# A residual kept turned in four PSUM banks through 32 expert steps of a decoder trunk

## The reference, cut to what matters

```python
h = h + y @ w_out
h = h + moe(rmsnorm(h, g_ffn), w_r, b_r, w1, b1, w2, b2)
gate = sigmoid(rmsnorm(h, g_ple) @ w_pg + b_pg)
h = h + gate * (p @ w_pp)                  # p: 256 per token
y_out = rmsnorm(h, g_final)

def moe(xt, ...):                          # top 4 of 32 experts
    combine = softmax_of_top4(xt @ w_r + b_r)
    for e in range(32):
        hdn = xt @ w1[e] + b1[e]           # 1024 -> 2048
        act = (clip(up) + 1) * min(gate, 7) * sigmoid(1.702 * gate)
        out += combine[:, e] * (act @ w2[e] + b2[e])   # 1024 -> 1024
```

## Time and profile before

| what | value |
|---|---|
| median of 3 runs | 1093.55 us (1091.79 to 1093.87) |
| the profiled execution | 1091.18 us, its span 1089.5 us |
| PE busy | 97% of the span |
| DVE, ACT, POOL busy | 35%, 15%, 1% |
| moved by DMA | 426.80 MB, mean 392 GB/s |
| mean granted clock of PE | 0.998 of full speed |

### The profile page before, as it was taken

The page is one execution under the profiler, slowest core; times in us unless marked ns, Lnnn a source line. Parts: engine busy times, 40 slices in busy tenths (PEclk is TensorE's granted clock), DMA queues, the critical chain, the costliest instruction groups (busy, mean ns, idle before and its releaser), DMA issues.

```text
span 1089.5 us, 13468 instructions
## 1 busy us (share of the span) xinstructions
PE 1061.2 (97%) x5250; PEld 429.7 (39%) x5250; DVE 385.1 (35%) x875; ACT 168.2 (15%) x298; POOL 13.8 (1%) x20
## 2 busy tenths in 40 slices
PE   9999999999999999999999999999999999999996
PEld 7884433444333333333333333333333333333342
DVE  6563743222333333333333333333333332333326
ACT  2550600010000000000000000000000000000034
POOL 0100200000000000000000000000000000000000
PEclk9999999999999999999999999999999999999999
DMA  9957699998999999999999999999999999999941
GB/s 281 354 216 300 262 401 428 424 397 374 395 431 430 433 431 433 430 428 434 427 432 433 426 434 425 432 430 431 431 437 426 434 430 431 433 422 430 423 182 40
DMA packets 34312, 426.80 MB, mean 392 GB/s; under 512 B 5383, under 2 KB 8655, under 8 KB 16493
## 3 DMA queue, kind: packets, MB, share of 16 engines
q1 hardware_dynamic: 34284, 426.41, 93.6%
HBM read 424.57 MB, written 1.43 MB: 391 GB/s over the span
## 4 chain that ended last, share of the span: by engine, by line
PE 76%; DMA 22%; DVE 1%; ACT 0%; SPq 0%; issue 0%; DVEq 0%
PE bank L1669 29%; DMA ring<-in_w 21%; PE bank L1710 17%; PE bank L1344 5%; PE bank L1599 5%; PE bank L1581 3%; PE bank L1432 3%; PE bank L1607 2%; PE bank L1592 2%; PE bank L1689 2%; PE bank L1767 1%; PE bank L1779 1%; DMA w_in<-in_w_in 1%; PE bank L1695 1%; PE bank L1654 1%; PE bank L1534 1%
## 5 line engine op out<-in xcount | busy, mean ns | idle before, releaser
L1669 PE MATMUL bank<-ring,xgT 128*64 128x512 f32 x2048 | 447.5, 593 | 14.5 <-DMA ring<-in_w 14.5
L1669 PEld LDWEIGHTS bank<-ring,xgT 128*64 128x64 f32 x2048 | 145.5, 137 | 298.3 <-issue 267.6
L1710 PE MATMUL bank<-ring,actT 128*64 128x512 f32 x1024 | 233.6, 598 | 0.0
L1177 DVE TENSOR_SCALAR gmin<-bank 128x512 f32<-128x512 f32 x32 | 22.1, 692 | 338.9 <-PE bank L1669 338.9
L1710 PEld LDWEIGHTS bank<-ring,actT 128*64 128x64 f32 x1024 | 67.9, 136 | 141.4 <-issue 120.5
L700 ACT ACTIVATE sig<-gmin 128x512 f32<-128x512 f32 x32 | 20.1, 630 | 446.4 <-DVE gmin L1177 446.4
L1131 DVE TENSOR_TENSOR h<-bank,h 128x512 f32<-128x512 f32 x132 | 84.8, 684 | 8.7 <-PE bank L1599 7.6
L1085 DVE TENSOR_TENSOR xgT<-bank,vecT 128x512 f32<-128x512 f32 x32 | 22.1, 692 | 155.9 <-PE bank L1592 155.2
L1171 DVE TENSOR_SCALAR wpick<-slot_no,pos,share 128x128 f32<-128x128 f32 (+1 forms) x96 | 27.1, 339 | 112.5 <-PE bank L1669 112.5
L1599 PE MATMUL bank<-y,wpickT 64*128 64x512 f32 x264 | 65.6, 615 | 0.8 <-ACT y L711 0.8
L711 ACT ACTIVATE y<-bank 128x512 f32<-128x512 f32 x32 | 19.1, 597 | 237.5 <-PE bank L1710 237.5
(11 more groups left out here) (306 smaller groups left out, 645.6 us busy)
## 6 DMA issues: line engine op xcount, KB each, us to landing
ring<-in_w SPq DMA_DIRECT2D x53, 4096.0 KB, 32.0
ring<-in_w SPq DMA_DIRECT2D x86, 2048.0 KB, 28.4
w_in<-in_w_in SPq DMA_DIRECT2D x3, 2048.0 KB, 14.2
w_out<-in_w_out SPq DMA_DIRECT2D x1, 4096.0 KB, 17.0
w_pg<-in_w_pg SPq DMA_DIRECT2D x4, 1024.0 KB, 26.7
h<-in_x_prompt SPq DMA_DIRECT2D x2, 512.0 KB, 3.9
w_in<-in_w_in SPq DMA_DIRECT2D x2, 512.0 KB, 7.8
w_in<-in_w_in SPq DMA_DIRECT2D x1, 1024.0 KB, 10.8
```

Of the source, the lines that this page charges most:

```text
L1669: ins = pe.matmul(bank[part][r, :], xgT[:, (k % FOUR) * W1_QUADS + k // FOUR, :], w[:, c:c + HALF], start=False, stop=(k == W1_SLOTS - 1), ...
L1710: ins = pe.matmul(bank[2][CAP * m:CAP * (m + 1), :], actT[:, half:half + CAP], pair[:, c:c + HALF], start=(f == 0), stop=(f == FF // P - 1 ...
```

## The change: the residual turned, in PSUM

What it does. At step 0 PE turns the prompt's residual by 16 plain matmuls with the identity (`residual_in`) into banks 4 to 7: channels on the partitions, eight blocks of 128, two blocks of 256 tokens in a bank. These banks stay open: each later `scatter` has `y` as the stationary operand (128 channels wide) and `wpickT` moving (256 tokens), eight matmuls that accumulate onto the residual. The eight samples are turned by `samples_in` and kept in SBUF (`hT_samples`); their products, eight matmuls of 8 columns, go to free columns of banks 0 and 2, and DVE adds them there (two additions of 128x32), for which PE waits ahead of the second matrix. The embedding is made turned, after step 3 alone, in eight blocks of 264 tokens. The gate is made turned: `w_pg` is the stationary operand, `tail_nT` moves, eight blocks. `b_pg` and `g_final` become columns of `vecT` (two more short loads at the start). The final norm's sums over channels are reduced by DVE over blocks and by PE over partitions; the rows are turned back at the end by 24 transposes (`turn_back`) into banks that have come free, and ACT and DVE scale them by the token's factor as they evict.

```diff
-    GATE_BANKS = (0, 2, 4)
+    GATE_BANKS = (0, 1, 2, 0, 1, 0, 1, 0)
+    GATE_BEFORE = (None, None, None, 0, 1, 3, 4, 5)
-    EMBED_STEPS = (2, 3)
+    EMBED_STEP = 3
+        def residual(b):
+            return bank[RESIDUAL + b // 2][:, (b % 2) * SEQ:(b % 2 + 1) * SEQ]
 # SP
-            load(bpg[:], a["b_pg"][0].partition_broadcast(P), rows_in)
-            load(gfin[:], a["g_final"].partition_broadcast(P), rows_in)
 # ACT, step
                 act.wait_ge(wpick_turned, i + 2)
-                act.wait_ge(spread, i * NT + NT)
+                act.wait_ge(spread, i * 2 + 2)
+                act.wait_ge(h_added, i + NT + 2)
                 act.activation(wpickT[:], bank[0][:, 0:T], ACT.Copy).then_inc(wpickT_ready, 1)
...
+                    act.activation(y[:, left], bank[2][:, left], ACT.Copy).then_inc(y_ready, 1)
+                    act.activation(y[:, right], bank[2][:, right], ACT.Copy).then_inc(y_right_ready, 1)
 # ACT, tail
+            for j in range(2):
+                act.wait_ge(spread, n * 2 + 1 + 3 * j)
+                for b in (2 * j, 2 * j + 1):
+                    act.activation(tail_nT[:, b, 0:SEQ], residual(b), ACT.Identity, scale=vcol("g_ple", b))
+            for j in (0, 1, 2, 3):
+                act.activation(squares[:, 2 * j:2 * j + 2, 0:SEQ], bank[RESIDUAL + j][:]..., ACT.Square)
+            for b in range(KD - 1):
+                sigmoid_of(b)
+                if b > 0:
+                    square_and_scale(b - 1)
+            square_and_scale(KD - 2)
+            sigmoid_of(KD - 1)
...
 # DVE, step
-                add_tile(0, P, 4, i * NT + 1, i * 2 * NT + NT)
-                add_tile(1, P, 6, i * NT + 2, i * 2 * NT + NT + 2)
+                add_samples(i * 2 + 2, i + NT + 1)
                 if not last:
                     make_xgT(i + 1, gathered_turned)
-                add_samples(4, i * NT + 3, i * 2 * NT + NT + 4)
 # DVE, add_samples
+                dve.tensor_tensor(samples_wide[:, 0:four], bank[0][:, T:T + four], samples_wide[:, 0:four], ALU.add)
+                dve.tensor_tensor(samples_wide[:, four:], bank[2][:, 0:four], samples_wide[:, four:], ALU.add
+                                  ).then_inc(h_added, 1)
 # DVE, tail
+            dve.tensor_reduce(token_sums[:, 0, :], squares[:].rearrange("p b t -> p t b"), AX.X, ALU.add)
+            link(dve.reciprocal(rstd_wide[:], rstd_wide[:]))
+            def normal(b):
+                dve.wait_ge(plegate_made, b + 1)
+                dve.tensor_tensor(gate[:, b, :], bank[GATE_BANKS[b]][:, 0:T], rstd_wide[:], ALU.mult)
+            def add_embedded(b):
+                dve.wait_ge(plegate_ready, b + 1)
+                link(dve.tensor_tensor(gate[:, b, :], gate[:, b, :], pwT[:, b, :], ALU.mult))
+                dve.tensor_tensor(gate[:, b, SEQ:T], gate[:, b, SEQ:T], hT_samples[:, b, :], ALU.add)
+                dve.tensor_tensor(gate[:, b, 0:SEQ], gate[:, b, 0:SEQ], residual(b), ALU.add).then_inc(h_final, 1)
+            for b in range(KD - 1):
+                normal(b)
+                if b > 0:
+                    add_embedded(b - 1)
+            add_embedded(KD - 2)
+            dve.tensor_reduce(token_sums[:, 1, :], squares[:, 0:KD - 1, :].rearrange("p b t -> p t b"), AX.X, ALU.add)
+            normal(KD - 1)
+            add_embedded(KD - 1)
...
 # PE
-                    ins = pe.matmul(bank[first_bank + m][0:rows, :], wpickT[r, t * P:t * P + rows], y[r, :],
-                                    start=True, stop=True)
+            def residual_in():
+                for b in range(KD):
+                    for t in range(2):
+                        pe.matmul(residual(b)[:, t * P:(t + 1) * P], h[:, t, b * P:(b + 1) * P], ident[:],
+                                  start=(b % 2 == 0 and t == 0), stop=False, skip_group_check=True)
+            def scatter(blocks=range(KD // 2), last=False):
+                for c in blocks:
+                    for m in range(2):
+                        r, b = slice(CAP * m, CAP * (m + 1)), KD // 2 * m + c
+                        ins = pe.matmul(residual(b), y[r, c * P:(c + 1) * P], wpickT[r, 0:SEQ], start=False, stop=last,
+                                        skip_group_check=True)
+            def scatter_samples(blocks=range(KD // 2)):
+                for c in blocks:
+                    for m in range(2):
+                        r = slice(CAP * m, CAP * (m + 1))
+                        at_c = (0 if m else T) + c * NS
+                        ins = pe.matmul(bank[2 * m][:, at_c:at_c + NS], y[r, c * P:(c + 1) * P], wpickT[r, SEQ:T],
+                                        start=True, stop=True, skip_group_check=True)
 # PE, step
+                if type(i) is int and i == EMBED_STEP + 1:
+                    pe.wait_ge(pw_ready, KD)
...
-                pe.wait_ge(h_added, i * 2 * NT + NT)
-                scatter(0, P, 4)
-                scatter(1, P, 6)
+                if started:
+                    samples_in()
+                    residual_in()
+                scatter()
...
-                pe.wait_ge(h_added, i * 2 * NT + NT + 2)
                 for t, rows in TILES:
                     ins = pe.transpose(bank[0][:, t * P:t * P + rows], wpick[0:rows, t, :], ident[0:rows, 0:rows])
                 ins.then_inc(wpick_turned, 1)
-                scatter_samples(4)
+                scatter_samples()
+                pe.wait_ge(h_added, i + NT + 2)
                 pe.wait_ge(actT_ready, i + 1)
 # PE, tail
+            scatter(range(2), True)
+            scatter_samples()
+            scatter(range(2, 4), True)
+            for b in range(KD):
+                for j, k in enumerate((0, 4, 1, 5, 2, 6, 3, 7)):
+                    ins = pe.matmul(bank[GATE_BANKS[b]][:, 0:T], w_pg[:, k, b * P:(b + 1) * P], tail_nT[:, k, :],
+                                    start=(j == 0), stop=(j == KD - 1), skip_group_check=True)
```

More of the change, by code:

```diff
@@ L782, in _ @@
+            act.wait_ge(rows_back, 2 * KD)
+            for m in range(2):
+                ins = act.activation(y_out[0:NS, 2, halves(m)], bank[BACK_BANKS[2][m]][0:NS, :], ACT.Copy,
+                                     scale=rstd[0:NS, 2:3])
+            ins.then_inc(y_final, 1)
         @block.vector
@@ L1123, in _, with add_samples @@
                 make_shares(r)
-            def add_tile(t, rows, first_bank, products, added):
+            samples_wide = hT_samples[:].rearrange("p k s -> p (k s)")
+            def add_samples(products, added):
                 dve.wait_ge(spread, products)
                 dve.wait_ge(h_added, added)
-                for m in range(2):
-                    src = bank[first_bank + m]
-                    dve.tensor_tensor(h[0:rows, t, halves(m)], src[0:rows, :], h[0:rows, t, halves(m)], ALU.add
-                                      ).then_inc(h_added, 1)
@@ new lines, in _ @@
+            dve.tensor_scalar(scaled[:, KD - 1, :], gate[:, KD - 1, :], vcol("g_final", KD - 1), None, ALU.mult
+                              ).then_inc(scaled_dve, 1)
+            dve.wait_ge(rms_ready, 6)
+            link(dve.reciprocal(rstd[:, 0:2], rms[:, 0:2]))
+            dve.wait_ge(rms_ready, 7)
+            dve.reciprocal(rstd[0:NS, 2:3], rms[0:NS, 2:3]).then_inc(rstd_ready, 1)
+            dve.wait_ge(rows_back, 2 * KD - 1)
+            for t in range(2):
+                dve.tensor_scalar(y_out[:, t, halves(1)], bank[BACK_BANKS[t][1]][:], rstd[:, t:t + 1], None, ALU.mult
+                                  ).then_inc(y_right_final, 1)
@@ new lines, in scatter @@
+            def scatter(blocks=range(KD // 2), last=False):
[4 more added lines that the diff above has]
+                                        skip_group_check=True)
+                        if last and c % 2:
+                            ins.then_inc(spread, 1)
+                if not last:
+                    ins.then_inc(spread, 1)
@@ L1771, in _ @@
[L1771 to L1781 removed]
+            pe.wait_ge(h_added, n + NT + 1)
@@ new lines, in _ @@
+            turn_back(5)
+            turn_back(6)
+            pe.wait_ge(h_final, 6)
+            for b in range(4):
+                turn_back_samples(b)
+            pe.wait_ge(plebias_ready, KD)
+            for b in range(4, KD - 1):
+                turn_back_samples(b)
+            pe.wait_ge(sums_ready, 2)
+            last_sums(token_sums[:, 1, :], True)
+            pe.wait_ge(sums_ready, 3)
+            last_sums(squares[:, KD - 1, :], False).then_inc(last_sums_made, 1)
+            turn_back(KD - 1)
```

408 lines of the change are left out of this document (170 added, 238 removed).

## The result

The changed kernel takes **1096.74 us** (median of 8 runs, 1095.57 to 1098.61), the kernel before beside it 1094.05 (8 runs): ratio 1.0028, 95% interval 1.0017 to 1.0039. A second set of runs gave 1096.23 against 1093.35, ratio 1.0029 (1.0019 to 1.0040). So it is slower by 2.7 to 2.9 us, a little over what can be told from no change. The forecast was 1095.0, range 1090.5 to 1104.0.

A forecast was written before the change was run, and what follows sets the result against it. PE was taken to bound early steps, the 430 GB/s weight stream from step 5 on, carrying early lateness. Loop +4.8 and tail -3.3 give +1.5 us on the median of 1093.55: 1095.0, range 1090.5 to 1104.

The forecast's parts named there:

- d: Time the change adds to each PE step: scatter -0.1, samples -0.05, new wait +0.8, together 0.65 us (0.4 to 0.9).
- Single work: Steps 0 to 3: residual and samples' turns add 5.1 us, the embedding saves 3.55, so 1.55 us later.
- The loop's end: Last step starts 4.8 us later by the weight stream: 1.55 + 5 x 0.65; 4.7 by PE.
- 5d: PE's added time per step, counted for five early steps only, carried by the weight stream to the loop's end: 5 x 0.65.
- rival C: In mid-step, short products' halves don't pair: about 1124 us (samples), 1146 (scatter), 1175 (both); chance 0.05.
- rival B: PE bounds every step once its added time exceeds the slack of 0.65 us; 1099.7 at 0.8, 1104.5 at 0.95; chance 0.22.
- The tail: From the copy of the last y to the end: 47.7 us before, 44.4 forecast, 3.3 sooner.
- The overhang of 2.2: DVE's work between gate blocks 6 and 7, 6.1 us with a reduction; block 7 covers 3.9, 2.2 stick out.
- rival E: Tail reductions reading 264 elements apart are slow; at twice the time per element, 2.1 us more, 1097.1; chance 0.09.
- The finish: Work after the last gate block, from normalisation through evictions to store and end: 8.7 us.
- D: Faster: the finish falls under the last gate block, the tail saves 7.3 us, 1091.0; chance 0.17.
- the frame: Kernel before's median of 1093.55 us, 2.4 above its profiled execution of 1091.18; the forecast was put on that median.

The follow-up runs named there:

- the runs with doubled products: Kernel before with the samples' products of every step made twice, both halves (1104.0 us, ratio 1.0092) or one half only (1103.0 us, ratio 1.0087).
- the run with 0.22 us added: Kernel before with two of the three turns of the next `wpick` made twice in every step: 1094.55 us, ratio 1.0010.
- the running sum: Changed kernel with the last reduction replaced by DVE adding each block's square to a sum between gate blocks: 1094.40 us, ratio 1.0007 to the kernel before.
- filled wait: Changed kernel with one more matmul between the samples' products and PE's wait for DVE's additions: 1097.19 us, ratio 1.0029 to the kernel before.
- late start: Kernel before with five more filler matmuls ahead of step 0: 1098.11 us against 1093.28, ratio 1.0045.

## Why the prediction was right

The direction, the size within 1.8 us and the main path were right: lateness of the first steps, carried by the stream, against a shorter tail. Point by point:

**The step, d = 0.65: measured 0.60.** The scatter saved nothing where 0.1 was expected; the samples run in pairs (1.02 against 0.96), as the runs with doubled products show from the other side (264 products on alternating halves took 62.3 us, 198 with two of three on one half 62.0). The wait was laid out at 0.8 with its first weight load; idle time is 0.48 to 0.56, since the second addition starts 0.11 us behind the first and not 0.2. The Trainium skill's rule on weight loads (TensorE: Matmul & The Clock Gate, LDWEIGHTS (loading the stationary operand)) gave an estimate of 1.7 us for the sixteen in series; the trace has 1.02, so they were not in series. The Trainium skill (TensorE: Matmul & The Clock Gate, Part 3: Packing small matmuls — row/col tiling, The mechanism) tells that products on different row groups overlap, and the trace agrees with its 1.02.

**Single work and the first five steps: 4.8, measured 4.45** (step 5 against step 0, 153.71 against 149.27), of it 1.45 of single work, where 1.55 was laid out, and 5 x 0.60.

**The loop's end was mis-sized: 4.8, measured 7.05 to 9.25.** The term that failed is 5d. It should have been some 8d to 9.5d: the run with 0.22 us added shows 1.70 from step 0 to the last step (884.78 against 883.08), 7.7 x 0.22; moving the samples gave 8.8 x 0.78; and the changed kernel itself has 7.05 - 1.45 = 9.3 x 0.60. Two of the steps more are shown: they lie behind the last wait for the ring, where PE's own pace counts again (0.43 more in the run with 0.22 added; in the running sum 1.26 more, 2.1 x 0.60). The rest, one step in the run with 0.22 added and 2.4 in the running sum (its last wait for the ring ends 686.71 us after step 5's start, before 685.26), is lateness that the stream takes on after step 5's start. The prediction's own row had this: DMA still idles in 280 to 290 us, which is inside step 5, and yet only the steps ahead of it were counted; after the change the share there is 0.72, before it 0.83. How many steps have a part in it was not taken apart. With 1.55 + 8.5 x 0.60 the forecast of the loop's end would have been 6.65. (The times given for rival C are one to three us above its own formula, 1122.8 for d = 1.55; nothing hangs on it.)

**Two bounds of equal length.** From step 5 to the last step the stream needs 736.5 to 736.8 us in this loop (running sum and filled wait, whose chains go through the ring late in the loop), PE 26 x 28.2 = 733.2 and 1.7 more for each fall of the clock. With two falls PE needs 736.6 and the second profile has 736.67; with three, 738.3, and the first profile has 738.36. So falls cost nothing up to two and 1.7 us for the third. This is rival B at its point of decision: d came out at 0.60 against a slack of 0.65, and falls of the clock, which no rival named, carried one profile over it. The sixteen executions of the changed kernel on record fit: thirteen with a mean granted clock of 0.993 to 0.997 have spans of 1093.8 to 1095.1, the three with 0.990 to 0.992 have 1096.5 to 1096.9.

**The tail: 3.3 saved, measured 1.7 and 2.0.** Gate start (3.4) and last block (33.5) came out at 3.3 and 33.55. The overhang of 2.2 came out at 2.5, of two errors that nearly cancel, which is luck: DVE's additions and ACT's scaling were shorter than laid out, and the reduction 1.4 longer than 2.06, as rival E had it. The Trainium skill's warning there (SBUF — State Buffer, Door 1: The DMA port swizzle) was borne out: 1.87 ns an element against 1.12 in order. The finish took 9.7 to 10.0 where 8.7 was laid out, the term of the tail that was mis-sized: ACT evicts four times in a row, 2.4 us, and not 1.8, and the samples' store stands behind four others, so that 3.3 us and not 2.5 lie between the last eviction and the end. D, the rival of a finish that hides, was off in the same place.

**What evened it out: the frame.** 7.05 later at the last step and 2.15 sooner from there to the end make the 4.9 us between the spans 1094.4 and 1089.5, but the medians differ by 2.8. The other 2 us lie in the kernel before: its profiled execution is 2.9 us under its median. Three profiles of its variants (late start, both runs with doubled products) show a fall of the clock behind the samples' embedding, of 1.6 us in two (36.67, and 37.52 less the 0.86 added, from step 2 to step 3, against 35.04 before) and 3.2 in the third (39.15 less 0.86); the profile of before has none. A fourth variant, with two turns made twice, shows none, and its profiled execution, too, is 2.0 us under its median. The changed kernel doesn't make that piece, and neither of its profiles falls there. The record has span and mean granted clock of 57 more executions of the kernel before: three of 1089.5 to 1089.7 us have 0.997, thirteen of 1090.5 to 1091.2 have 0.996, and of the 41 from 1091.3 to 1093.4 all but two have 0.994 or 0.995. So the longer executions of that kernel lost clock, and nearly all lost some that the profiled one (0.998) did not; that they lost it behind the samples' embedding is argued from the three profiles, since a mean doesn't tell the place. So errors of 2.2 in the loop and 1.2 in the tail, both to the same side, were more than halved by a term that the prediction didn't know. That the forecast came within 1.8 us is in that part luck.

## What to carry to other kernels

Where a stream of weights and an engine run close together, a delay in each early step counts until the stream's last idle time, and again behind the engine's last wait for the stream: count both ends, and don't take the larger of two nearly equal bounds as the sum. A short product that another engine must take in before PE goes on belongs as early in the step as its operands allow, with PE's independent work behind it; that order was worth 6.5 us here, more than the whole change cost. Before a reduction over an outer axis is put ahead of the last block, add it up as the pieces arrive.

## What the runs showed of the hardware

The granted clock of PE fell to the 1.2 GHz level inside a loop whose PE is busy 97%: after 0.5 us without work behind sixteen matmuls of 8 columns, in one to three of 32 steps in each of four profiles, at a cost of 1.5 to 1.7 us each; with the gap filled or moved away, none of four profiles showed one in the loop. In the variant without samples it fell after waits of PE for the ring (1.93 us up to 615.93, then 0.50 at 618 to 620 us); the version with the samples early waited for the ring twelve times, up to 1.62 us, without a fall. Behind 32 matmuls of 8 columns (L1524, 3.79 us), or still among them, it fell with no gap at all, in three of five profiles of kernels that make them. The Trainium skill tells of short idle stretches between groups of matmuls that make the clock swing (TensorE: Matmul & The Clock Gate, A second HAM failure mode: psum-queue depth-cycling); the trace agrees for the falls behind the wait of 0.5 us, while the falls with no gap lie outside what it tells.
